# Blocked inversion of 64x64 unit-triangular matrices in a Trainium2 layer kernel: products and updates over half the columns

## The reference, cut to what matters

```python
def step(S, inp):
    r_t, w_t, k_t, v_t, kk_t, b_t = inp
    sa = jnp.einsum('bhij,bhj->bhi', S, kk_t)
    S = S * w_t[:, :, None, :] - sa[..., None] * b_t[:, :, None, :] + v_t[..., None] * k_t[:, :, None, :]
    return S, jnp.einsum('bhij,bhj->bhi', S, r_t)
```

## Time and profile before

| | us |
|---|---|
| median of 3 runs | 3418.22 |
| lowest and highest | 3412.5 and 3419.65 |
| the profiled execution's own time | 3424.28 |
| its span, first to last instruction | 3422.6 |

### The profile page before, as it was taken

One profiled execution on the slowest core, in us unless ns is written; L12 is line 12 of the kernel. 1 busy time (PEld: TensorE's weight loads), 2 busy tenths in 40 slices (PEclk: granted clock), 3 DMA queues, 4 the chain that ended last, 5 costly groups with the idle time before them and its releaser, 6 DMA issues.

```text
span 3422.6 us, 85381 instructions
## 1 busy us (share of the span) xinstructions
PE 3217.8 (94%) x35488; PEld 2457.2 (72%) x35488; DVE 1912.4 (56%) x3612; ACT 940.3 (27%) x1635; POOL 268.4 (8%) x340
## 2 busy tenths in 40 slices
PE   5899999999999999999999999999998999999997
PEld 1356655665566556655666566999997999999997
DVE  1136555655565556555655535444436888887444
ACT  1122222222222222222222104233335444443333
POOL 0000000000000000000000001100001333332000
PEclk8899999999999999999999899999999999999999
DMA  8421212121212121212121225455544555554553
GB/s 323 195 93 65 83 68 75 57 85 66 77 56 83 68 77 56 82 69 76 57 84 43 89 88 191 147 173 177 177 160 138 182 184 178 178 183 155 179 179 138
DMA packets 66156, 413.62 MB, mean 121 GB/s; under 512 B 8176, under 2 KB 10864, under 8 KB 25328
## 3 DMA queue, kind: packets, MB, share of 16 engines
q1 hardware_dynamic: 65136, 407.51, 33.8%
q0 software_dynamic: 768, 2.10, 0.2%
HBM read 405.38 MB, written 4.19 MB: 120 GB/s over the span
## 4 chain that ended last, share of the span: by engine, by line
PE 84%; DVE 8%; issue 3%; DMA 2%; ACT 2%; SPq 0%; ACTq 0%; DVEq 0%; PEldq 0%
PE PB L620 16%; PE Q L857 5%; PE Q L859 5%; PE Q L858 5%; PE Q L747 5%; PE Q L734 4%; PE Q L753 3%; PE PB L857 3%; PE PB L858 3%; PE PB L859 3%; PE CH L857 3%; PE CH L858 3%; PE CH L859 3%; DMA ring<-w_mod_dram 2%; PE PB L605 2%
## 5 line engine op out<-in xcount | busy, mean ns | idle before, releaser
L620 PE MATMUL PB<-hT,ring 128*128 128x512 f32 (+1 forms) x1536 | 701.0, 561 | 5.4 <-PEq L609 5.4
L1527 DVE TENSOR_TENSOR w_lo_r<-ring,w_hi_r 128x1536 fp32r<-128x1536 f32 (+3 forms) x178 | 388.0, 2180 | 223.2 <-ACT w_hi_r L1133 223.1
L1133 ACT ACTIVATE w_hi_r<-ring 128x2048 fp32r<-128x2048 f32 (+2 forms) x178 | 312.2, 1754 | 483.7 <-PE Q L859 239.1
L620 PEld LDWEIGHTS PB<-hT,ring 128*128 128x128 f32 x1536 | 248.9, 189 | 122.2 <-issue 75.4
L747 PEld LDWEIGHTS Q<-arena 64*64 64x64 f32 x5120 | 161.7, 135 | 121.4 <-issue 121.4
L858 PE MATMUL PB<-hT_r,w_hi_r 128*128 128x256 f32 x832 | 236.0, 284 | 0.0
L857 PE MATMUL PB<-hT_r,w_hi_r 128*128 128x256 f32 x704 | 203.2, 289 | 5.7 <-DVE hT_r L1614 5.7
L1441 DVE TENSOR_TENSOR arena<-arena,Q 128x512 f32<-128x512 f32 x160 | 109.8, 686 | 176.2 <-PE Q L753 167.7
L857 PE MATMUL Q<-ff_hi_r,w_hi_r 128*128 128x256 f32 x704 | 202.7, 288 | 3.7 <-DVE w_lo_r L1687 2.7
L734 PEld LDWEIGHTS Q<-arena 64*64 64x64 f32 x5120 | 157.6, 135 | 62.9 <-issue 62.9
L857 PE MATMUL CH<-hT_r,w_hi_r 128*128 128x256 f32 x704 | 200.7, 285 | 0.0
(11 more groups left out here) (258 smaller groups left out, 6805.8 us busy)
## 6 DMA issues: line engine op xcount, KB each, us to landing
ring<-w_mod_dram SPq DMA_DIRECT2D x96, 1024.0 KB, 5.2
ring<-w_up_dram SPq DMA_DIRECT2D x88, 1024.0 KB, 4.9
ring<-w_rkv_dram SPq DMA_DIRECT2D x48, 1024.0 KB, 4.9
ring<-w_down_dram SPq DMA_DIRECT2D x64, 704.0 KB, 4.1
ring<-w_ga_dram SPq DMA_DIRECT2D x16, 1024.0 KB, 4.9
ring<-w_gb_dram SPq DMA_DIRECT2D x16, 1024.0 KB, 4.9
ring<-w_pa_dram SPq DMA_DIRECT2D x16, 1024.0 KB, 4.9
ring<-w_out_dram SPq DMA_DIRECT2D x16, 1024.0 KB, 5.0
```

The costliest lines, as they stand in the source:

```text
L620: last = mm(PB[slot % 2][:, 0:cols], tile(n, kt), hT[:, kt, 0:cols], start=(kt == 0), stop=(kt == KT - 1))
L1133: f(w_hi_r[:, r % 2, 0:n], ring[:, r, 0:n], ACT.Copy).then_inc(hi_rdy, 1)
L1527: tt(w_lo_r[:, r, 0:n], ring[:, r, 0:n], as_f32(w_hi_r[:, r % 2, 0:n]), ALU.subtract).then_inc(lo_rdy, 1)
```

## The change

Where a level with blocks of `b` updates the inverse, only every other block of `b` columns can change: the odd ones of `ZU` and the even ones of `ZL` for direction 0, and the other way round for direction 1. The new helper `part(v, b, odd)` is a strided view of these 32 of 64 columns. The moving operands of the three products, their results in the banks (now packed, 256 columns instead of 512) and every VectorE operation on them take only these columns. The weight tiles stay 64x64.

`TU` is no longer one buffer per direction in `arena`, but a tensor `tuz` with a buffer for each level and direction, zeroed once by VectorE ahead of the first pair (4608 elements in each partition), since its other columns are still loaded as weights by the third product. The last level's product is not used as weights and is packed. The columns of `ZU` and `ZL` that the first step no longer writes hold unit columns: GpSimd copies them from `eye2`, four copies for each pair, ahead of its `KR` copies, with a new semaphore `eye_rdy` on which TensorE and VectorE wait ahead of the levels. Some later scratch moves from `arena` into `tuz`, and the program is built with 2048 bytes of DMA scratch. In the changed file lines 734, 747, 753, 1421, 1424, 1428, 1429, 1436, 1441 and 1444 are 767, 782, 789, 1458, 1461, 1465, 1466, 1477, 1484 and 1488.

```diff
--- before.py
+++ after.py
@@ -33,7 +33,7 @@
 NCONST = 14
 QUAD = P // 4
 BODY_STEPS = 65
-ARENA = 32100
+ARENA = 30720
 RMS_EPS = 1e-6
 LNX_EPS = 64e-5
 LN_EPS = 1e-5
@@ -124,6 +124,14 @@
         gcol = sb("gcol", P, KT, 2)
+        tuz = sb("tuz", P, 2 * (LEVELS - 2) * TT + 2 * T)
+        def tuz_view(n, *shape):
+            d, lv = n // LEVELS, n % LEVELS
+            at = d * (LEVELS - 2) * TT + lv * TT if lv < LEVELS - 2 else 2 * (LEVELS - 2) * TT + d * T
+            return tuz[:, at:at + shape[0] * shape[1]].rearrange("p (a b) -> p a b", a=shape[0])
         top = [0]
         def view(*shape):
@@ -158,7 +166,9 @@
         NL = [view(NCH, C) for _ in range(2)]
         ZU = [view(NCH, C) for _ in range(2)]
         ZL = [view(NCH, C) for _ in range(2)]
-        TU = [view(NCH, C) for _ in range(2)]
+        TU = [[tuz_view(d * LEVELS + lv, NCH, C) for lv in range(LEVELS - 2)] + [tuz_view(d * LEVELS + LEVELS - 2, NCH, C // 2)]
+              for d in range(2)]
+        tu_last = [TU[d][LEVELS - 2] for d in range(2)]
         XT = [view(NCH, P) for _ in range(2)]
         VU = [view(NCH, 2, C) for _ in range(2)]
         gT = view(T)
...
@@ -413,6 +424,25 @@
             return (s + 4) % NCH if d == 0 else NCH - 1 - s
+        def part(v, b, odd):
+            names = "p n two b" if len(v.shape) == 2 else "p c n two b"
+            w = v.rearrange(("p " if len(v.shape) == 2 else "p c ") + "(n two b) -> " + names, two=2, b=b)
+            return w[:, :, odd, :] if len(v.shape) == 2 else w[:, :, :, odd, :]
+        def packed(v, b):
+            return v[:, 0:T].rearrange("p (c n b) -> p c n b", c=NCH, b=b)
+        def spread(v, b):
+            return v[:, None, :, :].to_broadcast([v.shape[0], NCH, C // 2 // b, b])
+        U_ODD, L_ODD = (1, 0), (0, 1)
         def wide(v, n):
             return v[:, None, :].to_broadcast([P, n, v.shape[-1]])
@@ -724,14 +754,17 @@
                 pe.wait_ge(nl_sb, i * 2 + 2)
                 pe.wait_ge(bonv_rdy, i + 1)
                 pe.wait_ge(g_rdy, i + 1)
+                pe.wait_ge(eye_rdy, i * 4 + 4)
                 for lv in range(LEVELS - 1):
+                    b = 2 << lv
                     for d in range(2):
                         pe.wait_ge(z_rdy[d], i * LEVELS + lv + 1)
                         small()
                         for ch in range(NCH):
+                            to = slice(ch * C // 2, (ch + 1) * C // 2)
                             for h in range(2):
                                 hr = slice(64 - 64 * h, 128 - 64 * h)
-                                last = mm(Q[2 * d][hr, ch * C:(ch + 1) * C], NL[d][hr, ch], ZU[d][hr, ch],
+                                last = mm(Q[2 * d][hr, to], NL[d][hr, ch], part(ZU[d][hr, ch], b, U_ODD[d]),
                                           start=True, stop=True)
                         last.then_inc(tu_ps[d], 1)
                     if more >= 1:
@@ -742,15 +775,18 @@
                         pe.wait_ge(tu_sb[d], i * (LEVELS - 1) + lv + 1)
                         small()
                         for ch in range(NCH):
+                            to = slice(ch * C // 2, (ch + 1) * C // 2)
                             for h in range(2):
                                 hr = slice(64 - 64 * h, 128 - 64 * h)
-                                last = mm(Q[2 * d + 1][hr, ch * C:(ch + 1) * C], ZL[d][hr, ch], TU[d][hr, ch],
-                                          start=True, stop=True)
+                                t = TU[d][lv][hr, ch]
+                                last = mm(Q[2 * d + 1][hr, to], ZL[d][hr, ch],
+                                          part(t, b, U_ODD[d]) if lv < LEVELS - 2 else t, start=True, stop=True)
                         if lv < LEVELS - 2:
                             for ch in range(NCH):
+                                to = slice(ch * C // 2, (ch + 1) * C // 2)
                                 for h in range(2):
                                     hr = slice(64 - 64 * h, 128 - 64 * h)
-                                    last = mm(Q[2 * d][hr, ch * C:(ch + 1) * C], TU[d][hr, ch], ZL[d][hr, ch],
+                                    last = mm(Q[2 * d][hr, to], TU[d][lv][hr, ch], part(ZL[d][hr, ch], b, L_ODD[d]),
                                               start=True, stop=True)
                         last.then_inc(zz_ps[d], 1)
                         if lv and d == 1:
@@ -1416,32 +1452,40 @@
                         last.then_inc(sc_sb, 1)
                     dve.wait_ge(sc_sb, i * 4 + 2 * d + 2)
+                    first = tu_last[d].rearrange("p c (n b) -> p c n b", b=1)
                     for h in range(2):
                         hr = slice(64 - 64 * h, 128 - 64 * h)
-                        m = V.tick(tt(TU[d][hr], SC[d][h][hr, :, 0],
-                                      off_mask[hr, d, 0, :][:, None, :].to_broadcast([64, NCH, C]), ALU.mult))
+                        m = V.tick(tt(first[hr], part(SC[d][h][hr, :, 0], 1, U_ODD[d]),
+                                      spread(part(off_mask[hr, d, 0, :], 1, U_ODD[d]), 1), ALU.mult))
                     V.need(m)
-                    flow(tt(ZU[d], wide(eye2[:, :], NCH), TU[d], ALU.subtract))
+                    flow(tt(part(ZU[d], 1, U_ODD[d]), spread(part(eye2[:, :], 1, U_ODD[d]), 1), first, ALU.subtract))
                     dve.wait_ge(nl_ps, i * 2 + d + 1)
                     tt(NL[d], chunks(Q[0][:, :]), wide(score_mask[:, 1 - d, 0:C], NCH), ALU.mult).then_inc(nl_sb, 1)
                     dve.wait_ge(nl_sb, i * 2 + d + 1)
-                    flow(tt(TU[d], NL[d], wide(off_mask[:, 1 - d, 0, :], NCH), ALU.mult))
-                    tt(ZL[d], wide(eye2[:, :], NCH), TU[d], ALU.subtract).then_inc(z_rdy[d], 1)
+                    flow(tt(first, part(NL[d], 1, L_ODD[d]), spread(part(off_mask[:, 1 - d, 0, :], 1, L_ODD[d]), 1), ALU.mult))
+                    tt(part(ZL[d], 1, L_ODD[d]), spread(part(eye2[:, :], 1, L_ODD[d]), 1), first,
+                       ALU.subtract).then_inc(z_rdy[d], 1)
                 if more >= 1:
                     outer(i + 1, 1, par_v)
+                dve.wait_ge(eye_rdy, i * 4 + 4)
                 for lv in range(LEVELS - 1):
+                    b = 2 << lv
                     for d in range(2):
                         dve.wait_ge(tu_ps[d], i * (LEVELS - 1) + lv + 1)
-                        tt(TU[d], chunks(Q[2 * d][:, :]), wide(off_mask[:, d, lv + 1, :], NCH), ALU.mult).then_inc(tu_sb[d], 1)
+                        to = part(TU[d][lv], b, U_ODD[d]) if lv < LEVELS - 2 else packed(tu_last[d].rearrange("p c t -> p (c t)"), b)
+                        tt(to, packed(Q[2 * d], b), spread(part(off_mask[:, d, lv + 1, :], b, U_ODD[d]), b),
+                           ALU.mult).then_inc(tu_sb[d], 1)
                     if more >= 1:
                         inputs(i + 1, 2 * lv)
                     for d in range(2):
                         dve.wait_ge(zz_ps[d], i * (LEVELS - 1) + lv + 1)
-                        last = tt(ZU[d], ZU[d], chunks(Q[2 * d + 1][:, :]), ALU.subtract)
+                        z = part(ZU[d], b, U_ODD[d])
+                        last = tt(z, z, packed(Q[2 * d + 1], b), ALU.subtract)
                         if lv < LEVELS - 2:
                             V.tick(last)
-                            last = tt(ZL[d], ZL[d], chunks(Q[2 * d][:, :]), ALU.subtract)
+                            z = part(ZL[d], b, L_ODD[d])
+                            last = tt(z, z, packed(Q[2 * d], b), ALU.subtract)
                         last.then_inc(z_rdy[d], 1)
                     if more >= 1:
                         inputs(i + 1, 2 * lv + 1)
@@ -1491,6 +1535,7 @@
                 dve.wait_ge(yr_free, i + 1)
                 tt(yr_out, ra, gT, ALU.mult).then_inc(pair_done, 1)
+            flow(nc.vector.memset(tuz[:], 0.0))
             fetch(par_v, 0)
             outer(0, 0, par_v)
             outer(0, 1, par_v)
@@ -1696,9 +1741,15 @@
         @block.gpsimd
         def _(pool):
+            pool.wait_ge(consts_ld, 16 * NCONST)
+            pool.sem_inc(seen, 1)
             with pool.Fori(0, PAIRS) as i:
                 pool.wait_ge(pair_done, i + 1)
+                pool.sem_inc(seen, 1)
+                for d in range(2):
+                    for z, odd in ((ZU[d], L_ODD[d]), (ZL[d], U_ODD[d])):
+                        nc.gpsimd.tensor_copy(part(z, 1, odd), spread(part(eye2[:, :], 1, odd), 1)).then_inc(eye_rdy, 1)
                 pool.wait_ge(x_rdy, i * 2 + 2)
                 pool.sem_inc(seen, 1)
                 for d in range(2):
@@ -1843,7 +1894,7 @@
     import concourse.bacc as bacc
     from concourse.bass_utils import run_bass_kernel_spmd
-    nc = bacc.Bacc("TRN2", target_bir_lowering=False, num_devices=1)
+    nc = bacc.Bacc("TRN2", target_bir_lowering=False, num_devices=1, dynamic_dma_scratch_size=2048)
     arrays = host_layout({k: np.asarray(v) for k, v in inputs.items()})
```

7 lines of the change are left out of this document (4 added, 3 removed).

## The result

| | before | changed |
|---|---|---|
| median of 9 runs each, on one chip | 3419.59 us | 3446.91 us |
| lowest and highest | 3412.5 and 3425.95 | 3429.78 and 3483.22 |
| ratio, with 95% interval | | 1.0075 [1.0052, 1.0099] |
| profiled execution, own time | 3424.28 | 3446.91 |
| its span, granted clock over it | 3422.6, 0.970 | 3445.2, 0.956 |

The account below looks back on a forecast made before the run. TensorE, busy for 94% of the span, was taken to bound the kernel; 0.82 us per pair, 13 us in 16 pairs, took the profiled 3424.3 us to 3411, and 6.1 us less for the median gave 3405 us, range 3376 to 3427.

Parts of the forecast that it names:

- Small matmuls: TensorE's 28 inversion groups per pair: halved moving columns save 0, as weight loads set the pace; 27 us as far end.
- The term that stood for the clock: TensorE's lower clock at pairs' starts: shifted pairs may gain or lose 1.3 us, some six of them, 8 us either way.
- the prediction's own signs of being wrong: Groups of lines 767, 782, 789 closer than 0.9 us, halved operations much over 0.42 us, or TensorE waiting inside the levels.
- The rival that ended on the slower side: Strided VectorE operations in the first step at 1.38 us, twice full price: 56 us lost, 3474 us; chance 10%.
- The first step: Inversion's first step, direction 1: halved VectorE operations bring TensorE's group 0.60 us earlier per pair; 0.05 us charged for GpSimd's copies.
- The levels: Halved masks and updates: only the last update counts, shortening TensorE's wait at line 797 by 0.27 us per pair.
- The sum: 0.60 + 0.27 - 0.05 = 0.82 us per pair, 13 us in 16 pairs.

Follow-up runs that it names:

- run 2: Kernel before, with only the moving operands cut to the first 32 contiguous columns from the second level on (22 of 28 groups): 3417.13 us, 0.9991.
- run 5: Changed kernel with the 1 MB load of the r weights issued in the chunk loop instead of ahead of the levels: 3395.81 us, 0.9927.
- run 6: Changed kernel with 64 moving columns again in 26 of 28 groups and the r weights' load moved into the chunk loop: 3396.73 us, 0.9937.
- run 12: Kernel before with only the change's levels (32 columns, halved masks and updates), old first step, r weights' load moved into the chunk loop: 3440.27 us, 1.006.
- run 7: run 5's kernel plus a deliberate TensorE wait ahead of the second line 664, for seven GpSimd copies, in every looped pair: 3709.09 us, 1.0868.
- Run 11: Kernel before with only the change's new first step (32 columns, GpSimd unit columns), old levels with 64 moving columns, load in place: 3411.29 us, 0.9976.
- Run 15: run 12's kernel with the first level back on 64 columns: 3403.36 us, 0.9952.
- run 9: Kernel before with only the r weights' load moved into the chunk loop: 3417.01 us, 0.9993.
- run 10: Changed kernel without its new first step and GpSimd copies, so the levels alone, load in place: 3440.86 us, 1.0065.
- run 1: Changed kernel with 64 moving columns again in 26 of 28 groups, VectorE's halved work kept, load in place: 3402.54 us, 0.995.

## Why the prediction was wrong

**The step that failed** is the first one, "Small matmuls. ... I take 0 for the 28 groups". It read the pace of the weight loads, and the pace was right: 0.061 us for two loads, groups of 0.96 us where wide ones take 0.98, and runs 2, 5 and 6 show that halved columns are worth nothing that a measurement can tell at full clock. But it took the granted clock inside the levels for given. With half the columns moving on the same loads, idle times ahead of the groups (1.5 to 2.1 us in the change, 0.3 us in run 12) left TensorE at half its clock for 23.9 us or more. The pages of the kernel before could not show this, since every group there has 64 columns. They did show that the clock goes low behind a wait and comes back (at the pairs' starts), and a change that leaves TensorE the same time for half the columns should have had a rival in which it does not come back: four such pairs cost 45 us, and run 7 shows up to 44.4 us of low clock in one pair. The term that stood for the clock, 8 us to either side, counted only the pairs' starts. And among the prediction's own signs of being wrong stood that TensorE waits inside the levels: it did, in four pairs, for 1.5 to 2.1 us.

**Slower, for another reason.** The rival that ended on the slower side priced strided VectorE operations at 1.38 us. They took 0.42 us. Its 10% stood on the wrong engine.

**The first step**: 0.60 us per pair forecast, 0.05 us of it to be given back. Run 11, which has it alone, is 0.24% [0.15%, 0.33%] faster, 8 us or 0.5 us per pair, as forecast, with some waits on the fetch in it.

**The levels**: 0.27 us per pair, 4.3 us, forecast. Run 15 against run 9, both with the load moved and the old first step, gives 13.6 us. The traces show most of the surplus of 9 us: the low clock at the pairs' starts and between them adds up to 61 us in pairs 0 to 13 of run 9, and 48 us in run 15, so 7 us less at half the clock. The prediction named this term and gave it no sign; here it fell on the good side. Some 2 us are not accounted for.

**The load and the fetch**: the prediction said that the load of the weights and the fetch of instructions stay where they are, by not naming them. "Nothing changes its place" holds for the streams, and not for the meeting of two transfers whose times hang on different engines. In pairs 7 to 9 of the kernel before the fetch ran in the middle of the load (20.3 to 21.2 us into the pair, the load from 18.3 or 19.5 on for 5 us), and TensorE didn't wait. In its pairs 1 and 10 it ran when the load was all but over (21.8 and 21.4 us), and TensorE waited for 1.2 and 0.65 us. In the changed kernel it ran just ahead of the load in pairs 7, 9 and 11 (18.0 to 19.4 us) and at its very end in the four pairs that stood still (22.1 us in pairs 8 and 10). Which it is hangs on a microsecond.

**The sum**: without the clock in the levels the change is worth 21.2 us (run 5 against run 9, 0.6%), where 13 us were forecast. Most of the surplus lies in the term that the prediction left without a sign, so hitting it would have been luck: the low clock at the pairs' starts adds up to 48 us in the trace of run 5 and to 61 us in that of run 9, and 13 us less at half the clock are 7 of the 8 us. With the clock in the levels, the change costs 27 us.

**What stays open.** Why a wait of 0.3 us takes the clock down in three pairs of run 12 and not in the other eleven was not tried apart. Nor was whether the count of moving columns or their stride holds it down. Nor was what else would bring it back, such as large matmuls put behind the wait. Single projections with 512 columns (lines 661, 664, 650) stand among the narrow groups in each low stretch and don't bring it back alone. But all 22 stretches of 23.9 us or more in pairs 0 to 13 (four in the change, one in run 10, three in run 12, fourteen in run 7) ended in one kind of place: while the modulation product and the projection right behind it (lines 582 and 650 in the change) ran, or at most 0.8 us behind them. In nine of them, the 44.4 us of run 7, this pair of groups had passed once without effect. The runs of the change spread over 53 us, where those of run 5 spread over 10; that the number of such pairs differs from run to run fits this. Only one run of each has a trace, but the granted clock of every run is on record, and it goes with the time: 0.962 at 3429.78 us, 0.956 at 3446.91 and 0.946 at 3483.22, the run left out of the ratio. Between the first and the last that is about 115 us more at half the clock, worth 57 us, where the times differ by 53. In the last pair a low clock of 34.1 us was seen in run 2's trace too, in the chunk loop, against 13.7 us in the kernel before. It began at a wait of 2.7 us for a load, and the work in it has 64 moving columns, with a group of 512 (line 645) for each chunk and waits of 0.2 us. So 64 columns alone don't always bring the clock back.

## What to carry to other kernels

Where the weight loads set TensorE's pace, fewer moving columns saved nothing, and they can cost: behind an idle time the clock may stay at half, so look up how long the granted clock stays low behind each wait before thinning the matmuls out, and leave the columns wide in the groups right behind a wait. When a change has shifted a stream by a microsecond, look at the instruction queue's packets beside the large loads. And VectorE can be spared its half of the columns while TensorE still moves them all: run 1 has most of the gain (17 of some 21 us), and little of the risk.

## What the runs showed of the hardware

- A group of 16 float32 matmuls on 64x64 weights takes 0.96 us with 32 moving columns at the full clock and 0.98 us with 64. At half the clock it takes 1.7 to 1.8 us with either.
- Behind a wait of 2.6 us the low clock lasted 3.4 to 6.8 us with 64 contiguous columns in the groups that follow (and didn't come in 2 of 14 pairs), and 23.9 to 44.4 us with 32 strided ones. The Trainium skill, in TensorE: Matmul & The Clock Gate, HAM oscillation, warns of gaps longer than any that stood in the levels here; the low clock in run 12 began behind 0.31 us. Here the measurement decides: shorter idle times were enough where narrow groups followed. The same page of the Trainium skill, What's actually happening, says that the clock is set by how busy the engine has been recently; the profile has TensorE busy without a gap in the low stretches too (23.90 of 23.90 us), so the busy share doesn't show whether the two widths (3.4 to 6.8 us against 23.9 to 44.4 us) agree with that.
- In the change, where the instruction queue's packet (0.02 MB) came at the end of a 1 MB load, TensorE stood still for 1.5 to 2.1 us (four pairs). Where it ran with the load's start, no wait was seen (ten pairs).
- VectorE's operation on 256 elements took 0.42 to 0.43 us in the mean also where it reads or writes every second float32 on 128 partitions (lines 1461, 1465, 1466), and 0.47 us on 64 (line 1458).
